# One level of Strassen's product over half the depth of the gate and up projections, with the third of its four weight differences made by GpSimd

## The reference

```python
D_FF = ((8 * D_MODEL // 3 + 255) // 256) * 256      # 5632 = 11 x 512
...
y = _rms(h, norm_ffn_g[i])
h = h + (jax.nn.silu(y @ w_gate[i]) * (y @ w_up[i])) @ w_down[i]
```

## Time and profile before

| quantity | value |
|---|---|
| time, median of three runs | 2114.72 us (2114.6 to 2115.41) |
| span of the profiled execution, first to last instruction | 2112.9 us |
| the profiled execution's own time | no separate figure is given; the span stands 1.8 us below the median |
| TensorE busy | 2099.0 us, 99% of the span |
| VectorE busy | 1215.2 us, 58% |
| ScalarE busy | 902.5 us, 43% |
| GpSimd busy | 21.1 us, 1% (all of it memsets of one column and the issuing of transfers) |
| mean granted TensorE clock | 0.998 of full speed |

### The profile page before, as it was taken

One profiled execution on the slowest core, in us unless ns is written; L12 is line 12 of the kernel. 1 busy time (PEld: TensorE's weight loads), 2 busy tenths in 40 slices (PEclk: granted clock), 3 DMA queues, 4 the chain that ended last, 5 costly groups with the idle time before them and its releaser, 6 DMA issues.

```text
span 2112.9 us, 24852 instructions
## 1 busy us (share of the span) xinstructions
PE 2099.0 (99%) x10595; PEld 1786.0 (85%) x10595; DVE 1215.2 (58%) x1214; ACT 902.5 (43%) x861; POOL 21.1 (1%) x40
## 2 busy tenths in 40 slices
PE   9999999999999999999999999999999999999998
PEld 8888888888888888888999888888888888888887
DVE  5576555665544544456889755444445454454555
ACT  5444444544343443345353444334333433334443
POOL 2000000000000000000000000000000000000000
PEclk9999999999999999999999999999999999999999
DMA  8655555555555555665655556565555555555553
GB/s 246 224 177 170 177 160 183 176 179 163 196 193 187 198 190 188 199 239 184 205 191 163 179 180 200 183 193 186 199 191 187 187 191 199 186 193 183 194 200 120
DMA packets 224733, 398.34 MB, mean 189 GB/s; under 512 B 11202, under 2 KB 56506, under 8 KB 224368
## 3 DMA queue, kind: packets, MB, share of 16 engines
q1 hardware_dynamic: 221344, 387.64, 56.4%
q0 software_dynamic: 2528, 8.00, 1.2%
q10 hardware_dynamic: 752, 1.12, 0.1%
HBM read 394.62 MB, written 2.12 MB: 188 GB/s over the span
## 4 chain that ended last, share of the span: by engine, by line
PE 95%; DVE 4%; ACT 1%; DMA 0%; issue 0%; ACTq 0%; SPq 0%
PE psA L478 27%; PE psA L480 27%; PE psA L479 27%; PE psA L543 6%; PE psA L547 3%; DVE CA L1464 1%; PE psB L600 1%; DVE lo L1260 1%; DMA X<-in_x_dram 0%; PE psB L698 0%; PE psB L724 0%; PE psB L646 0%; PE psB L758 0%; ACT hi L868 0%; PE psB L685 0%
## 5 line engine op out<-in xcount | busy, mean ns | idle before, releaser
L1260 DVE TENSOR_TENSOR lo<-raw,hi 128x2048 fp32r<-128x2048 f32 (+2 forms) x368 | 834.8, 2272 | 619.8 <-ACT hi L868 617.7
L868 ACT ACTIVATE hi<-raw 128x2048 fp32r<-128x2048 f32 (+2 forms) x368 | 697.9, 1899 | 684.3 <-PE psA L480 592.7
L478 PE MATMUL psA<-hi,XHL 128*128 128x512 f32 x1632 | 637.9, 391 | 0.0
L480 PE MATMUL psA<-hi,XHL 128*128 128x512 f32 x1632 | 633.9, 388 | 0.0
L479 PE MATMUL psA<-lo,XHL 128*128 128x512 f32 x1632 | 633.4, 388 | 0.0
L480 PEld LDWEIGHTS psA<-hi,XHL 128*128 128x128 f32 x1632 | 306.4, 188 | 63.6
L478 PEld LDWEIGHTS psA<-hi,XHL 128*128 128x128 f32 x1632 | 306.5, 188 | 62.6 <-DVE lo L1260 0.4
L479 PEld LDWEIGHTS psA<-lo,XHL 128*128 128x128 f32 x1632 | 306.6, 188 | 61.7
L478 PE MATMUL psA<-hi,YH 128*128 128x512 f32 x608 | 237.2, 390 | 0.0
L480 PE MATMUL psA<-hi,YL 128*128 128x512 f32 x608 | 236.6, 389 | 0.0
L479 PE MATMUL psA<-lo,YH 128*128 128x512 f32 x608 | 236.6, 389 | 0.0
(11 more groups left out here) (353 smaller groups left out, 1273.4 us busy)
## 6 DMA issues: line engine op xcount, KB each, us to landing
raw<-in_w_in_dram SPq DMA_DIRECT2D x158, 1024.0 KB, 5.1
raw<-in_w_gate_dram SPq DMA_DIRECT2D x44, 1024.0 KB, 5.1
raw<-in_w_up_dram SPq DMA_DIRECT2D x44, 1024.0 KB, 5.2
raw<-in_w_down_dram SPq DMA_DIRECT2D x44, 1024.0 KB, 5.1
raw<-in_w_out_dram SPq DMA_DIRECT2D x32, 1024.0 KB, 5.1
raw<-in_w_branch_dram SPq DMA_DIRECT2D x16, 1024.0 KB, 5.0
raw<-in_w_ple_gate_dram SPq DMA_DIRECT2D x16, 1024.0 KB, 5.0
raw<-in_w_in_dram SPq DMA_DIRECT2D x16, 512.0 KB, 4.7
```

The lines of the kernel that those rows point to most:

```text
L478: e.matmul(dst, A2[0], B2[0], start=first, stop=False, skip_group_check=True)
L480: return e.matmul(dst, A2[1], B2[0], start=False, stop=last, skip_group_check=True)
L868: e.activation(hi[u % H][:, 0:m], raw[u % R][:, 0:m], ACT.Copy).then_inc(hi_made, 1)
L1260: e.tensor_tensor(lo[u % R][:, 0:m], raw[u % R][:, 0:m], hi[u % H][:, 0:m].bitcast(F32), ALU.subtract).then_inc(lo_made, 1)
```

## The change

In each of the 11 blocks the upper half of the depth (rows 0 to 1023) of gate and up together is one 2 x 2 by 2 x 2 block product: the token halves and two depth quarters of `y` on one side, the two depth quarters of `w_up` and `w_gate` on the other. It is now made from 7 products of blocks in place of 8 (Strassen's scheme in Winograd's form). The lower half of the depth stays an ordinary product. A block is one group of kind "S" with 11 units in the order of `STEPS`. The seven units a, x, f, e, d, c, g have one product with 128 tokens, 12 matmuls; the four units p2, p3, p0, p1 have two, 24 matmuls. The seven weight operands are the loaded quarters a, c (up) and b, d (gate) and four differences: x = b - a, f = d - x, g = c - f, made by VectorE, and e = d - b, the third in the order of use, made by GpSimd in the place of b. The block's sums lie in the four banks of `psA`, called A, B, C and D, and partial sums are copied out by ScalarE in the middle of a block (`S1B`, `CG`, `SU3`), because later products go on adding to the same bank.

The four input differences (S1 to S4) are made once, by `input_forms` at unit 214. Buffers are given out by `fills` from 8 places: three more are found where `YH`, `YL` and the end of a work area lie, since the down product now follows each second block and needs only 8 of its 16 tiles. From unit 210 on the splits run 4 units ahead.

What `fills` gives out decides when each of a block's transfers can start. Counted in units from the block's first unit a, and the same in every block but the first, the place is free when this unit begins (0 is a itself, -1 the last unit ahead of the block):

| operand | a | b | d | p2 | c | g (its place only) | p3 | p0 | p1 |
|---|---|---|---|---|---|---|---|---|---|
| blocks 1 to 10 | -7 | -6 | -4 | -2 | -1 | 0 | +1 | +2 | +3 |
| block 0 | -5 | -4 | -2 | 0 | 0 | 0 | +1 | +2 | +3 |

```diff
+STEPS = ("a", "x", "p2", "f", "p3", "e", "d", "p0", "c", "g", "p1")
+SOURCE = {"a": (0, 0), "b": (1, 0), "c": (0, 4), "d": (1, 4), "p0": (0, 8), "p1": (0, 12), "p2": (1, 8), "p3": (1, 12)}
+FILLED = ("a", "b", "x", "d", "f", "p2", "c", "g", "p3", "p0", "p1")
+BANKS = ({"A": 0, "B": 3, "C": 1, "D": 2}, {"A": 1, "B": 0, "C": 2, "D": 3})
...
-    for j in range(11):
-        group(("fg", j), "N", A["w_gate_2"][0], 512 * j, K16)
-        if j in (4, 8):
-            down(range(j - 4, j), j // 4 - 1)
-        group(("fu", j), "N", A["w_up_2"][0], 512 * j, K16)
+    for j in range(0, 10, 2):
+        mixed(j)
+        mixed(j + 1)
+        down((j, j + 1), j // 2)
+    mixed(10)
...
+def fills(units):
+    free = [(0, n) for n in range(R)] + [(206, 7), (218, 5), (218, 6)]
...
+    def take(key, until, W=None, k0=0, nk=4, pieces=()):
+        free.sort()
+        after, slot = free.pop(0)
...
+            for role in FILLED:
+                until = u + STEPS.index("e" if role == "b" else role)
...
+                    take((g.name[1], role), until, g.W[n], k0, 4, [(g.cols, 512)])
...
 SyncE
+            for n in loads[2:]:
+                if after:
+                    e.wait_ge(unit_done, after)
...
 GpSimd
+            for j in range(11):
+                e.wait_ge(raw_landed[b], b_landed)
+                e.wait_ge(raw_landed[d], d_landed)
+                e.wait_ge(form_made, 3 * j + 1)
+                e.tensor_tensor(raw[b][:, :], raw[d][:, :], raw[b][:, :], ALU.subtract).then_inc(third_made, 1)
...
 TensorE, mixed(u)
+                elif role == "p2":
+                    if j == 0:
+                        e.wait_ge(flip_low, SECOND + 3)
+                        e.wait_ge(bank_dve, freed(("out2", 5 - LOWER)))
+                    elif j % 2:
+                        e.wait_ge(*up(j - 1, "t0"))
+                    block("D", 8, t1, first=True)
+                    e.wait_ge(*copied(j, "P5"))
+                    x = block("C", 8, t0)
...
 ScalarE, mixed(u) and its loop
+                if role == "a":
+                    e.wait_ge(unit_done, u + 1)
+                    if j:
+                        e.wait_ge(*up(j - 1, "hidden"))
+                    e.activation(S1B[:, :], quarter(j, "A"), ACT.Copy).then_inc(sum_copied, 1)
+                elif role == "x":
+                    e.wait_ge(unit_done, u + 1)
+                    if j:
+                        e.wait_ge(*up(j - 1, "hidden"))
+                    e.activation(CG2, quarter(j, "C"), ACT.Copy).then_inc(sum_copied, 1)
...
+                if g.kind == "S" and STEPS[i] == "x":
+                    mixed(u)
+                if u and u not in ATTEND and u not in EARLY:
+                    for n in ahead(u):
+                        split(n)
...
+                if g.kind == "S":
+                    if STEPS[i] != "x":
+                        mixed(u)
...
 VectorE, mixed(u), hidden(j) and its loop
+                if role == "a":
+                    arrived("a")
+                    arrived("b")
+                    form("x", "b", "a")
+                elif role == "x":
+                    arrived("d")
+                    form("f", "d", "x")
+                elif role == "f":
+                    arrived("c")
+                    form("g", "c", "f")
+                elif role == "d":
+                    e.wait_ge(third_made, j + 1)
+                split(u)
...
+                if u in ENDED:
+                    hidden(ENDED[u])
+                if u:
+                    for n in ahead(u):
+                        if units[n][0].kind == "S":
+                            mixed(n)
+                        else:
+                            split(n)
+                if u == SUMS:
+                    input_forms()
```

More of the change, by code:

```diff
@@ L143, in build_hybrid @@
         XH, XL = XHL[:, :, 0, :], XHL[:, :, 1, :]
-        YH = sb("YH", [128, 16, 256], F32R)
-        YL = sb("YL", [128, 16, 256], F32R)
+        for name in ("YH", "YL"):
+            with ExitStack() as here:
+                sb("below " + name, [128, UNIT], F32, here)
+                raw.append(sb("raw in " + name, [128, UNIT], F32, here))
+            with ExitStack() as here:
+                sb("under " + name, [128, UNIT], F32, here)
+                lo.append(sb("lo in " + name, [128, UNIT], F32R, here))
+            if name == "YH":
+                YH = sb("YH", [128, 16, 256], F32R)
+            else:
+                YL = sb("YL", [128, 16, 256], F32R)
+        PH, PL = YH[:, 4:6, :], YL[:, 4:6, :]
         ID = sb("ID", [128, 128])
@@ L307, in build_hybrid, with place, ahead, copied @@
         named = {g.name: g for g in groups}
[L308 to L311, removed]
+        places, hplaces, loads = fills(units)
+        def place(u):
+            g, i = units[u]
+            if g.kind != "S":
+                return places[u]
+            role = STEPS[i]
+            return places[g.name[1], "b" if role == "e" else role]
+        def ahead(u):
+            if u < FURTHER:
+                return (u + AHEAD,)
+            if u == FURTHER:
+                return (u + AHEAD, u + AHEAD + 1)
+            return (u + AHEAD + 1,) if u + AHEAD + 1 < n_units else ()
+        def copied(j, n):
+            return sum_copied, 4 * j + {"P1": 1, "P5": 2, "U2": 3, "U3": 4}[n]
+        def gate(j, n):
+            return gate_made, 3 * j + {"t1": 1, "t0": 2, "gated": 3}[n]
+        def up(j, n):
+            return up_made, 3 * j + {"t0": 1, "t1": 2, "hidden": 3}[n]
         def freed(name):
@@ L348, in build_hybrid @@
         TURN2 = {208 + 4 * f: f for f in range(4)}
-        TURN3 = {347 + 3 * f: f for f in range(4)}
-        TURNH = {named[("fu", j)].last + 2: j for j in range(11)}
+        BEGIN = [named["S", j].first for j in range(11)]
+        TURN3 = {named["down", 20].last + 2 + f: f for f in range(4)}
+        TURNH = {named["down", 2 * j - 2].first + 1 if j % 2 else BEGIN[j + 1] + 3 if j < 10 else named["proj", 2].last: j
+                 for j in range(11)}
+        ENDED = {named["S", j].last + 1: j for j in range(11)}
+        LOWER = 2 + named["out2", 2].pair
+        SUMS = 214
+        P_TURN = BEGIN[10] + 3
+        PLE = named["ple", 0].first + 1
         TAPS = [(j, c) for j in range(31) for c in range(2)]
@@ L536, in unit @@
                 if i == 0 and g.number >= 2:
[L537 to L538 removed]
+                    bank_free(g)
                 if g.kind == "T2":
@@ L827, in side @@
                     j = TURNH[u]
-                    e.wait_ge(bank_dve, freed(("fu", j)))
+                    e.wait_ge(*up(j, "hidden"))
                     e.wait_ge(flip_low, HIDDEN + j)
@@ L831, in side @@
                 if u in TURN3:
-                    e.wait_ge(bank_dve, freed(("down", 8 + TURN3[u])))
+                    e.wait_ge(bank_dve, freed(("down", 20 + TURN3[u])))
                     turn_h(THIRD + TURN3[u], TURN3[u])
```

384 lines of the change are left out of this document (300 added, 84 removed).

## The result

The changed kernel takes 2150.09 us (median of four runs, 2149.99 to 2150.53), the kernel before 2114.8 on the same chip (2114.6 to 2115.41, four runs): a ratio of 1.0167 [1.0153, 1.0182], 1.7% slower. The forecast was 2126 with a range from 2116 to 2145. The direction was right, the size was not. The profiled span is 2148.4 us, 35.5 more than in the earlier trace rows.

A forecast was written before the change was run, and what follows sets the result against it. TensorE was taken as the bound, busy 2099.0 of 2112.9 us. 2112.9 - 29.9 (matmuls) + 33.0 (copies) + 8.0 (entry) = 2124.0 of span, 1.8 below the median, so 2125.8, say 2126; range 2116 to 2145.

The forecast's parts named there:

- What goes: Over 11 blocks, 132 matmuls at 0.2267 us each go from TensorE: 29.9 us saved.
- The copies in the middle of a block: p2's second product waits for copies behind p3's late split: 3.0 us a block, 33.0 us in 11 blocks.
- Odd blocks: p2's first product waits 2.4 us for `hidden`, within the copies' wait, so 3.0 us stays the total.
- The entry: In block 0 p2's late place delays TensorE's second product by 11.0 us, 8.0 beyond the 3.0 counted.
- GpSimd: GpSimd's third difference takes 2.29 us, at a cost of 0; the rival of holding VectorE over 3.1 us got 8%.
- a full lock: GpSimd and VectorE exclude each other for GpSimd's whole 4.5 us instruction: 5 x 1.4 = 7 us more.
- The clock: Forecast kept TensorE's matmuls at their usual pitch behind the waits, adding nothing for a lower clock.
- the other case: Rival: the clock falls at the waits, giving 2141 us (half of the blocks) or 2156 (all); chance 22%.
- The rival that had it in all blocks: Half clock behind the wait in every block, 2.72 us each, 30 us, 2156; within the clock rival's 22%.
- a gap of 1.50: Sign against the clock rival: an early TensorE gap of 1.50 us left the matmuls behind it at their pitch.
- The rest: Twelve more sums on X of 1.2 us, beside down units with VectorE half free, counted as nothing.
- Faster, as the copies come in time: Rival: p3's split does not hold the copies up, leaving 22 us of waits, 2107 us; chance 11%.

The follow-up runs named there:

- e23: Changed kernel with ScalarE's copies of sums A and C ahead of p3's split and VectorE's `hidden` rows ahead of difference g and f's split: 2102.38 us, 0.9939.
- e2: Changed kernel with ScalarE's copies of sums A and C put ahead of its split of p3: 2127.99 us, 1.0064 against the kernel before.
- e3: Changed kernel with the three rows of `hidden` put ahead of difference g and the split of f on VectorE: 2138.84 us, 1.0109 against the kernel before.
- e1: Changed kernel with GpSimd's loop removed and VectorE making the third difference just ahead of its split of e: 2139.66 us, 1.0119 against the kernel before.
- e6: Changed kernel with useless matmuls into an unused bank just ahead of TensorE's two waits in p2: 2135.28 us, 1.0095 against the kernel before.
- e8: e23 with the sum on X ahead of VectorE's splits in the last four down groups: 2097.06 us, 0.9915 against the kernel before.

## Why the prediction was wrong, point by point

**What goes.** 29.9 us, confirmed by e23's account.

**The copies in the middle of a block.** The mechanism was right in each part: transfer at the start of x, split, two copies, second product. The size was 2.65 by the list, 2.8 counted from start to start, in place of 3.0: the transfer landed in 5.14 (1419.66 to 1424.80), and the next start behind a split comes 1.81 after its own, not 1.92. ScalarE's waits for `w_gate` grew from 8 us past the 55 forecast, since p3's split is reached early:

```profile
ACT hi L1123 <- DMA raw<-in_w_gate_dram: 106.8, 13, 10.2
```

**Odd blocks.** Right that the two waits lie within each other (e2, e3), and in the sum of 3.0. The split in 2.4 and 0.6 is e1's; with GpSimd S1B alone makes 3.3, and the copy is hidden behind it. All ten waits sum to 29.8 where 30.0 was forecast.

**The entry.** 9.7 in place of 11.0: the wait for X was 9.75 (forecast 10.0), but the further 1.0 for the copies didn't come: p2's first product ran at the low clock, and by its end they were done. The later landing that the prediction allowed for two transfers issued together, up to 2 us, did not come: p2's, issued at 1272.19 with another 0.4 us behind it, had landed by 1277.34.

**GpSimd.** Its row is 4.6 us, not the 2.29 taken, and the lock exists. The prediction priced a full lock at 5 x 1.4 = 7 us; against e1 it adds 5 x 1.1 in odd blocks, less the 2.8 that VectorE alone loses in block 0. The cost of about 0 was nearly right, but for a wrong reason: the instruction was not short, the idle time beside it took most of it.

**The clock: the step that failed.** The prediction chose full clock over the waits and gave the other case 22%. The clock was low behind every one of the eleven waits in blocks 0 to 10, and that took 17.3 us; e6 confirms the share of the ten. The rival that had it in all blocks priced a low half product at 2.72, 30 us in all; the low stretch ended after some eight matmuls, so it was 1.5 or 1.6 each. The evidence held against it, a gap of 1.50, was half as long as the waits in question, and that for it showed a fall 2.2 us after the last matmul. The nearer row was the second. The Trainium skill's account of such a loop (TensorE: Matmul & The Clock Gate, HAM oscillation) was the right warning; the trace agrees that each of the ten waits in p2 was followed by low matmuls, while e3 shows that a wait of 2.78 need not be.

**"The rest", counted at nothing: the second failure.** The twelve more sums on X were costed by VectorE's free share. Three of them close a ring in the last down groups, 4.4 us of waits, shown by e8.

Together: +11.1 was forecast; the clock adds 17.3, the ring 4.4, modelled ends and restarts 3.5, the stage's start 0.7; the entry takes off 1.3 and the ten waits 0.2. That is +35.5, the account above.

**The ways not taken.** "Faster, as the copies come in time" named the right condition and held back the gain that lay there: e23 meets it by the order rather than by a faster landing, and with the entry still in place runs in 2102.4.

## What to carry to other kernels

Before crediting removed matmuls, look for each new instruction that something of TensorE's waits for, and read what stands ahead of it on its engine: one late transfer there stops TensorE in every iteration, and moving two groups of instructions turned 1.7% slower into 0.6% faster. Where a change makes TensorE idle for 2 to 3 us at a time, count the matmuls behind each wait at half clock too, here 1.5 to 1.6 us a wait. An added instruction's place matters before its engine: the same subtraction cost 23 us more behind a late split than ahead of it.

## What the runs showed of the hardware that was not expected

- Waits of much the same length are followed by the low clock or not: those of 2.55 to 2.70 us in the changed kernel five times in five, those of 2.56 to 2.92 in e3 twice in ten, and the 3.32 of e2 three times in five. What decides is not shown; the length alone doesn't.
- The clock's fall can come after TensorE has gone back to work: in odd blocks it came behind the fourth matmul, about 1 us after the wait's end.
- Executions of the same kernel differ in it: e1's four took 2137.62 to 2145.09 us, with a mean granted clock of 0.994 in the three faster and 0.990 in the slowest.
- A GpSimd subtraction of 128 x 2048 float32 takes 4.6 us with no difference or split of VectorE's beside it, against VectorE's 2.28, and where it meets one of VectorE's differences it holds it for 3.8 us or 4.4.
- Useless matmuls in TensorE's waits made the kernel 14.8 us faster.
